# Two transformer blocks on one core: output projection, norm, row turning and router logits in one stage piped by token tile

## The reference, cut to what matters

```python
# first block (once)
x = x + memory_cross_attention(...)            # ends in  o @ w_o_x
x = x + hier_moe(rms_norm(x, g_moe), w_rg, b_rg, w_re, b_re, w_gate, w_up, w_down)
x = rms_norm(x, g_final)
# second block (twice), alpha = (2 * 2) ** 0.25
mix = _token_mixer(...)                        # ends in  merged @ w_o[l]
x = _layernorm(alpha * x + mix, ln1_g[l], ln1_b[l])
ffn = _hier_moe(x, ...)                        # logits: x @ w_rg + b_rg, x @ w_re + b_re
x = _layernorm(alpha * x + ffn, ln2_g[l], ln2_b[l])
```

## Time and profile before

| | before |
|---|---|
| median of 3 runs | 3120.4 us (3113.94 to 3122.73) |
| profiled execution, its own time | 3114.51 us |
| its span in the trace | 3112.7 us |
| PE busy | 2482.1 us, 80% |
| DVE busy | 1284.4 us, 41% |
| ACT busy | 881.6 us, 28% |
| POOL busy | 406.1 us, 13% |
| DMA | 565.77 MB, mean 182 GB/s |

### The profile page before, as it was taken

The page is one execution under the profiler, slowest core; times in us unless marked ns, Lnnn a source line. Parts: engine busy times, 40 slices in busy tenths (PEclk is TensorE's granted clock), DMA queues, the critical chain, the costliest instruction groups (busy, mean ns, idle before and its releaser), DMA issues. The chain is left out here.

```text
span 3112.7 us, 50456 instructions
## 1 busy us (share of the span) xinstructions
PE 2482.1 (80%) x18120; PEld 1949.6 (63%) x18121; DVE 1284.4 (41%) x2666; ACT 881.6 (28%) x1612; POOL 406.1 (13%) x716
## 2 busy tenths in 40 slices
PE   4975798868888886969899669983959989849882
PEld 3964678844444445847677657762848667747661
DVE  3437345232111115634653434335644744343334
ACT  2233234111111112144532213322233632213221
POOL 0000000022111210000000124432000000024333
PEclk9988899879999997979999869996979999959996
DMA  3200242389999954122121378994212212179993
GB/s 114 93 1 1 68 135 75 158 322 404 407 414 410 390 239 138 41 68 60 43 68 43 121 286 339 384 367 135 69 35 68 60 51 68 55 288 346 378 393 136
DMA packets 209256, 565.77 MB, mean 182 GB/s; under 512 B 26550, under 2 KB 170550, under 8 KB 184544
## 3 DMA queue, kind: packets, MB, share of 16 engines
q1 hardware_dynamic: 191056, 538.71, 46.7%
q0 software_dynamic: 18064, 25.23, 2.5%
HBM read 560.44 MB, written 36.18 MB: 192 GB/s over the span
## 5 line engine op out<-in xcount | busy, mean ns | idle before, releaser
L1020 PEld LDWEIGHTS ps<-r_gate_up,e_xT 128*64 128x64 f32 x2272 | 267.0, 144 | 92.3 <-issue 88.8
L1020 PE MATMUL ps<-m_gate_up,e_xT 128*64 128x256 f32 x1088 | 269.7, 411 | 61.9 <-DMA m_gate_up<-in_w_gate_up 48.0
L1020 PE MATMUL ps<-r_gate_up,e_xT 128*64 128x128 f32 x2272 | 279.1, 284 | 43.0 <-DMA r_gate_up<-in_w_exp_gate_up 28.5
L1022 PE MATMUL ps<-r_gate_up,e_xT 128*64 128x128 f32 x2272 | 279.3, 284 | 0.0
L1022 PE MATMUL ps<-m_gate_up,e_xT 128*64 128x256 f32 x1088 | 269.8, 411 | 0.0
L1020 PEld LDWEIGHTS ps<-m_gate_up,e_xT 128*64 128x64 f32 x1088 | 159.8, 149 | 174.2 <-issue 110.3
L1022 PEld LDWEIGHTS ps<-r_gate_up,e_xT 128*64 128x64 f32 x2272 | 267.0, 144 | 0.0
L1174 DVE TENSOR_TENSOR e_hid<-e_silu,ps 64x128 f32<-64x128 f32 (+1 forms) x210 | 70.1, 335 | 472.7 <-ACT e_silu L1062 467.9
L1062 ACT ACTIVATE e_silu<-ps 64x128 f32<-64x128 f32 (+1 forms) x210 | 63.8, 304 | 641.8 <-PE ps L1022 641.8
L455 POOL TENSOR_TENSOR all_x<-all_x,ln_rows 128x1024 f32<-128x1024 f32 x16 | 48.2, 3038 | 1263.7 <-DVE all_x L448 1263.7
L1921 PE MATMUL ps<-t_hT,t0a_t0g_w 128*128 128x512 f32 x768 | 199.4, 411 | 4.6 <-DVE t0a_t0g_w L1943 2.4
(11 more groups left out here) (605 smaller groups left out, 4740.1 us busy)
## 6 DMA issues: line engine op xcount, KB each, us to landing
m_gate_up<-in_w_gate_up SPq DMA_DIRECT2D x32, 4096.0 KB, 38.2
r_gate_up<-in_w_exp_gate_up SPq DMA_DIRECT2D x64, 2048.0 KB, 33.8
m_down<-in_w_down SPq DMA_DIRECT2D x32, 2048.0 KB, 37.9
r_down<-in_w_exp_down SPq DMA_DIRECT2D x64, 1024.0 KB, 34.7
t0a_t0g_raw<-in_w_in SPq DMA_DIRECT2D x32, 512.0 KB, 3.8
t1a_t1g_raw<-in_w_in SPq DMA_DIRECT2D x32, 512.0 KB, 3.8
mixw_raw<-in_w_in SPq DMA_DIRECT2D x10, 1024.0 KB, 5.4
xaw_raw<-in_w_kv_x SPq DMA_DIRECT2D x8, 1024.0 KB, 5.3
```

The lines of the kernel that those rows point to most:

```text
L1020: nc.tensor.matmul(ps_gu[q][0:SLOTS], xT[:, c, :], ring.gu[:, s, 0, c, span], start=c == 0, stop=c == DC - 1)
L1022: last = nc.tensor.matmul(ps_gu[q][SLOTS:P], xT[:, c, :], ring.gu[:, s, 1, c, span], start=c == 0, stop=c == DC - 1)
```

## The change

The projection, the norm, the turning and the router logits become one stage, `project_route`. The last weight chunk is walked tile by tile: DVE takes the statistics of each 256 columns right behind the add, and when a token tile's last columns are in, its row factors are worked out, ACT applies them, PE turns the tile, and ACT and DVE copy it out, four 128x128 pieces each, with the feature's gain (and bias) applied there as per-partition factors. PE then makes that tile's logits. In the second blocks `x` itself still needs gain and bias: DVE multiplies and POOL adds, per tile, beside this.

- The router's weights are allocated and loaded before the projection. The turned rows have a small tile of their own, so no ring slot is borrowed.
- The ring is allocated after this stage: no expert weight is loaded during it. At the start of `moe` SP issues all slots at once, 3 or 6.
- In the first block the normed rows are stored to DRAM in the new stage, tile by tile; in the second blocks the store stays at the start of `moe`, ahead of the ring's loads.
- `moe` starts with the logits already in PSUM (bank 4). The ranks go to bank 7.

```diff
@@ ExpertRing
     def load_first(self, sp):
-        for s in range(self.n - 1):
+        for s in range(self.n):
             for m in range(2):
                 self.load(sp, s, s, m)
@@ moe
             def _(sp):
-                sp.dma_start(rows_dram.rearrange("(t p) d -> p t d", p=P), h_rows).then_inc(rows_stored, 16)
-                sp.wait_ge(logits_ready, 1)
-                sp.wait_ge(rows_stored, 16)
-                for m in range(2):
-                    ring.load(sp, RING - 1, RING - 1, m)
+                if h_rows is not None:
+                    sp.dma_start(rows_dram.rearrange("(t p) d -> p t d", p=P), h_rows).then_inc(rows_stored, 16)
+                ring.load_first(sp)
                 sp.wait_ge(table_ready, 2)
@@
             def _(pe):
-                for t in range(TT):
-                    for c in range(DC):
-                        last = nc.tensor.matmul(ps[:, t, 0:NG + NE], hT[:, c, t * P:(t + 1) * P], router.w[:, c, :],
-                                                start=c == 0, stop=c == DC - 1)
-                last.then_inc(logits_ready, 1)
-
                 pe.wait_ge(hot_ready, 1)
@@ project_route, new: tensor
+                for c in range(n_chunks - 1):
+                    for t in range(TT):
+                        project(c, t)
+                for t in range(TT - 1):
+                    project(n_chunks - 1, t)
+                turn_rows(0)
+                project(n_chunks - 1, TT - 1)
+                for t in range(1, TT):
+                    turn_rows(t)
+                    route(t - 1)
+                route(TT - 1)
@@ project_route: scalar, behind the casts of the weights
+                def out(t):
+                    act.wait_ge(turned, t + 1)
+                    if t >= 2:
+                        act.wait_ge(routed, t - 1)
+                    for c in range(DC // 2):
+                        src = ps[:, 2 * (t % 2), c * P:(c + 1) * P]
...
+                for t in range(TT - 1):
+                    norm(t)
+                out(0)
+                norm(TT - 1)
+                for t in range(1, TT):
+                    out(t)
@@ project_route: vector
+                def add(c, t):
...
+                    vec.scalar_tensor_tensor(xs, xs, alpha, ps[:, i % 8, 0:WIDTH], ALU.mult, ALU.add).then_inc(summed, 1)
+                    dve.wait_ge(summed, i + 1)
+                    link(vec.bn_stats(stats[:, t, c, :], xs))
...
+                for t in range(TT):
+                    add(n_chunks - 1, t)
+                    factors(t)
+                    if t == TT - 2:
+                        out(0)
+                if finish is not None:
+                    dve.wait_ge(row_landed, 32)
+                for t in range(1, TT):
+                    out(t)
+                    scale(t)
@@ project_route: sync, behind the loads of weights, router and gain rows
+                if store is not None:
+                    for t in range(TT):
+                        sp.wait_ge(normed, t + 1)
+                        sp.dma_start(store[t * P:(t + 1) * P], rows(t)).then_inc(stored, 16)
+                    sp.wait_ge(stored, 16 * TT)
@@ program
-                ring = ExpertRing(nc, s3, i["w_gate_up"][0], i["w_down"][0], 512)
                 router = Router(s3, i["w_rg"][0], i["b_rg"][0], i["w_re"][0], i["b_re"][0])
...
+                cross_attention(nc, k, x, col, i, router, rows_dram)
...
+                ring = ExpertRing(nc, s3, i["w_gate_up"][0], i["w_down"][0], 512)
+                moe(nc, "e0", k, x, rows_dram, None, col("g_moe"), ring, router)
```

More of the change, by code:

```diff
@@ L318, in plain, with rms_rows @@
     return f
-def rms_rows(nc, name, parts, eps, loads=(), ring=None):
+def rms_rows(nc, name, parts, eps, loads=()):
     with Stage(nc, name) as st:
@@ L415, in post_norm @@
         r = st.sb("r", [P, 4, TT])
[L416 to L419, removed]
+        gain_landed, bias_landed, chain, mean_ready, root_ready, factors_ready, normed, scaled = (
+            st.sem(n) for n in ("gain_landed", "bias_landed", "dve_chain", "mean_ready", "root_ready", "factors_ready",
+                                "normed", "scaled"))
         with nc.Block() as block:
@@ L424, in _ @@
                 sp.dma_start(rows[:, 1], row_b.partition_broadcast(P)).then_inc(bias_landed, 16)
[L425 to L429, removed]
             @block.vector
@@ L454, in _ @@
                     pool.wait_ge(scaled, t + 1)
[L455 to L459, removed]
-                    for t in range(TT):
-                        pe.wait_ge(shifted, t + 1)
-                        for c in range(DC):
-                            last = nc.tensor.transpose(ps[:, 2 * t + c // 4, c % 4 * P:(c % 4 + 1) * P],
-                                                       x[:, t, c * P:(c + 1) * P], k["ident"][:])
-                        last.then_inc(full, 1)
+                    nc.gpsimd.tensor_tensor(x[:, t, :], x[:, t, :], rows[:, 1], ALU.add)
             @block.scalar
@@ L474, in _ @@
                                    bias=r[:, 3, t:t + 1]).then_inc(normed, 1)
[L475 to L479, removed]
 def final_norm(nc, name, x, row_g, eps):
@@ L819, in __init__, with moe @@
                       (self.bias[:, 0:NG], b_rg.partition_broadcast(P)), (self.bias[:, NG:], b_re.partition_broadcast(P))]
-def moe(nc, name, k, x, hT, h_rows, gain, ring, router, alpha=1.0):
+def moe(nc, name, k, x, rows_dram, h_rows, gain, ring, router, alpha=1.0):
     FF = ring.ff
@@ L1540, in cross_attention @@
+def cross_attention(nc, k, x, col, i, router, rows_dram):
     MT = i["mem"].shape[1] // P
@@ L1620, in _, with token_mixer @@
                 sca.activation(cs[:, 1], ang[:, 0], ACT.Sin)
-def token_mixer(nc, name, k, x, col, i, l):
+def token_mixer(nc, name, k, x, col, i, l, router, row):
     ps, vec, sca = k["ps"], nc.vector, nc.scalar
@@ L1852, in token_mixer @@
             branches.finish()
-        project_onto(nc, name + "o", k, hT, i["w_o_2"][l], x, alpha, Split(nc, merged, hT, 0.5))
+        finish = sx.sb("finish", [P, 2, D])
+        project_route(nc, name + "o", k, hT, i["w_o_2"][l], x, alpha, Split(nc, merged, hT, 0.5), router, 1e-5,
+                      lambda t: x[:, t, :], col(f"ln1_g{l}"), col(f"ln1_b{l}"),
+                      finish=(finish, row(f"ln1_g{l}"), row(f"ln1_b{l}")))
 class GatedBranches:
```

216 lines of the change are left out of this document (177 added, 39 removed).

## The result

The changed kernel took 3090.9 us in the median of 6 runs (3084.4 to 3098.9), the kernel before 3118.3 beside it on the same chip (3113.9 to 3122.7). The ratio is 0.9917, 95% interval 0.9903 to 0.9931. The profiled execution has a span of 3088.4 us, 24.3 less than before. Later, beside other kernels, the changed kernel gave 0.9930 (0.9917 to 0.9943).

What follows compares the result with a forecast made beforehand. Expert phases were taken as bound by DMA in `e0` and `e2` and by PE's start in `e1`. Terms -8.7, -17.7 and -4.4 gave -30.8 us, so 3083.7 or 3089.6, forecast as 3090, range 3070 to 3113.

Steps and rivals of the forecast that it cites:

- An expert phase ends at: issue of the first ring load + transfer work + DMA idle time.: Expert phases: law for their end while DMA is saturated behind the start; otherwise the end goes by PE's start.
- The idle 15.1 and 14.4 us: `e0` and `e2`, behind the early ring loads: idle DMA time before PE frees a slot, forecast to be given back.
- `e0` -8.7: First expert phase: ring load 11.6 later, idle 15.1 gone, rows' 5.2 transfer moved out, together -8.7 us.
- `e1` -17.7: Second expert phase: DMA could give back at most 18.6 us; PE's earlier start is the smaller gain, -17.7 us.
- E + 16: New stage's tail: last logit matmul E + 16.0 at the low clock, E + 10.6 at the high; E ends the projection.
- The 34.2 us: `e0` and `e1`: time from `moe`'s start to PE's first expert, with `e0`'s gather wait taken for both.
- `e2` -4.4: Third expert phase: first load 10 us later, idle 14.4 given back, DMA saturated from then on, -4.4 us.
- Nothing given back: Rival, all expert phases: early ring start lost and idle stretches stay, +26.5 us, 3147; chance 0.05.
- Gathers stuck behind the ring: Rival, expert phases: first gather waits until the ring is full, +11 us, 3132, from about 27 us landing; chance 0.07.
- PE's start governs everywhere: Rival, all expert phases: each ends earlier by PE's earlier start, -50 us, 3070; chance 0.12.
- Half the gain: Rival: the tail is longer or half of the idle time stays, -3 us, 3117; chance 0.14.
- The rule against it: Ring's first loads: issue a DMA early and wait late; loads 10 to 12 us later would make the change a loss.

Runs made afterwards that it cites:

- late_ring: Changed kernel, with the ring's first loads waiting for the chosen experts, 9.2 to 9.5 us later in each expert phase; ratio 0.9989 to the kernel before.
- late_experts: Changed kernel, with DVE clearing its landing tile five more times at each expert phase's start, delaying the experts but not the ring's loads; ratio 0.9982.
- before_late_ring: Kernel before, with the first ring loads issued at the expert phase's start, behind the rows' store, instead of at the norm's start; ratio 1.0055.
- the first five experiments: Five of the follow-up kernels, each an edited kernel with its own profile; the text does not list which five or give a joint time.
- second_only: Changed kernel with the new stage only in the two token mixers, the first block as in the kernel before; ratio 0.9959 to the kernel before.
- after_again: The changed kernel, no edit, run and profiled a second time to see how far one profile repeats; ratio 0.9930 to the kernel before.

## Why the prediction was right, and where its terms were off

The forecast was 3090, the median 3090.9; the sum was -30.8, the runs say -27.4 and the spans -24.3. The likeliest case came about by its own mechanism. That the number met within 1 us is luck: the sum was 3.4 us too large a gain, the median of the kernel before, 3120.4 over three runs then, is 3118.3 over six, and the errors in the sum's terms partly cancelled. "The trace shows each expert phase's first load 10 to 12 us later" was a forecast, no reading; it came 9.4 to 14.1 later, measured from each block's start.

- **"An expert phase ends at: issue of the first ring load + transfer work + DMA idle time."** Right as a law for `e0` and `e2`; `late_ring`, `late_experts` and `before_late_ring` show it to within the 2 to 3 us of a profile. The idle 15.1 and 14.4 us are gone.
- **`e0` -8.7: mis-sized.** The first load went out at 602.9 for 604.9, the first expert at 636.8 for 639.1, the share was 0.99 to 1.01 as forecast. With that start the same sum would be some -9.7, and the stretch gave -3.8 and -6.8. The failing step is "transfer work" as a sum of bytes over the mean rate: the median of the last load's increments came 12.0 us earlier than before, the last of the 16 only 4.6. That last engine lay 6.4 us behind the median in the profile of before, 13.8 in that of after, and 10.4 to 11.6 in the first five experiments. So the base that the sum stood on was itself a favourable draw, by some 4 us of lag or by the 2.0 that `second_only`'s unchanged `e0` took longer, and part of the term was never there to lose.
- **`e1` -17.7: mis-sized.** The rule "the smaller gain counts, PE's earlier start" held: -13.1 at the first expert, -10.9 and -13.0 at the end. PE's start itself was 4.6 us late, 4.0 of it by the stage's end, where 1787.6 was forecast and 1785.3 + 6.35 = 1791.7 came. The tail's upper bound of E + 16 was too low. I had walked the tail at either clock, but with no hold in it; the DVE step of "about 0.2" took 1.57 beside POOL, and with the clock's fall behind it the last logits ended at E + 18.5. The 34.2 us from the phase's start to the first expert were right (34.7).
- **`e2` -4.4: right** in the mean (-6.0, again -1.2), by a term that depends on the clock: where its tail fell to the low clock (+13.6 or +14.5 at the ring) the gain was gone.
- **The stretches' unchanged code** gave another -3.6 us that the sum didn't have, the mixers and the first half; `after_again` shows -1.9 there.
- **Nothing given back**: out, the share shows it. **Gathers stuck behind the ring**: out; the wait of 7.87 us in front of DVE's copy belongs to a gather that landed in 10 us (issued at 1807.0), where 27 decides. But the small version is real: DVE's wait for the first gather went from 3.21 to 7.87 in `e1`, which the 34.2 us had in. **PE's start governs everywhere**: true for `e1` alone. **Half the gain**: what `second_only`'s `e2` and the low-clock tails come near.
- **The rule against it** (issue early): 16 to 20 us of lead in a phase were worth 4 to 7 us, because the ring was full long before PE used it.

## What to carry to other kernels

Giving up an early prefetch costs only what it wasn't going to stand idle for: compare the time at which the buffers are full with the time at which the first one comes free, and shorten whichever is later; here the changed order brought them in `e0` from 11 us apart (ring full at 652, first refill at 663) to 7 the other way round (654 and 647), with a DMA share of 0.99 to 1.01 from there on. For a short latency-bound tail ask what the clock and the other engines do in it: the first block's tail took 10.7 us; a tiny DVE instruction with two SBUF tensors, held by a POOL operation, made that 12.2 in a second block, and the fall of PE's clock 18.5. And a base profile's stretch is a draw too: when a phase ends with the last of 16 DMA engines, take several profiles before crediting a change with 4 us.

## What I had not expected of the hardware

- DVE's 128x1 instruction with two SBUF tensors was held until POOL's 128x1024 operation ended (1.57 us for 0.16); with one tensor and a scalar operand it took 0.21 beside the same operation. DVE's 128x1024 multiplication took 1.22 us alone and 2.31 beside POOL. The Trainium skill, page "SBUF — State Buffer", section "SBUF: two separate sides", has DVE operations with two SBUF inputs and POOL's take a shared port pair in turn, each for its whole length; the runs agree.
- PE's granted clock fell from 1.00 to 0.50 in 18 of 24 tails, though PE was mostly busy in them and each gap was at most 1.6 us. It fell in the first or second tile's logits or right behind them. Tails with the same gaps kept the high clock, so what decides is open; six idle matmuls, 0.96 us, in each gap kept it high in 6 of 6.
- The 16 DMA engines finish one load within 0.5 to 0.9 us of one another in a saturated stream of plain loads, also beside full gathers and stores, and 16 to 22 us apart by the end of an expert phase. The cause is open.
- Single profiles of the same `e0` code differ by up to 5.5 us.
